# The last feed-forward's down projection as seven half-size products instead of eight, on one Trainium2 core

## What is computed

```python
h = rms_norm(x, norm_ffn[l])
x = x + (jax.nn.silu(h @ w_gate[l]) * (h @ w_up[l])) @ w_down[l]
```

## Time and profile before

| | us |
|---|---|
| median of three runs | 1574.17 |
| the profiled execution, first to last instruction | 1570.6 |
| PE busy in it | 1536.9 (98%) |
| DVE busy | 1007.2 (64%) |
| ACT busy | 832.5 (53%) |
| POOL busy | 210.5 (13%) |

### The profile page before, as it was taken

The page is one execution under the profiler, slowest core; times in us unless marked ns, Lnnn a source line. Parts: engine busy times, 40 slices in busy tenths (PEclk is TensorE's granted clock), DMA queues, the critical chain, the costliest instruction groups (busy, mean ns, idle before and its releaser), DMA issues.

```text
span 1570.6 us, 20022 instructions
## 1 busy us (share of the span) xinstructions
PE 1536.9 (98%) x7872; PEld 1247.3 (79%) x7872; DVE 1007.2 (64%) x1681; ACT 832.5 (53%) x1459; POOL 210.5 (13%) x278
## 2 busy tenths in 40 slices
PE   9999999999999999999989999999999999999999
PEld 8877777788877888888877766888778888888887
DVE  4267977865479998999787786575765333434231
ACT  5278776554456888888863434435434333333220
POOL 1000014522234000000062101111201000000000
PEclk9999999999999999999999999999999999999999
DMA  6122121114547999999943111031212323223232
GB/s 233 65 81 79 56 71 65 54 54 150 214 161 231 375 421 421 421 422 421 326 149 107 54 54 54 28 108 54 81 58 78 108 81 108 92 82 121 67 112 90
DMA packets 78641, 235.89 MB, mean 150 GB/s; under 512 B 6960, under 2 KB 9424, under 8 KB 66256
## 3 DMA queue, kind: packets, MB, share of 16 engines
q1 hardware_dynamic: 68288, 207.62, 36.3%
q10 hardware_dynamic: 6624, 14.88, 2.5%
q0 software_dynamic: 3632, 12.08, 2.0%
HBM read 221.97 MB, written 12.60 MB: 149 GB/s over the span
## 4 chain that ended last, share of the span: by engine, by line
PE 84%; DVE 11%; ACT 2%; issue 1%; DMA 1%; POOL 0%; SPq 0%; DVEq 0%; ACTq 0%; POOLq 0%
PE bank L109 80%; PE bank L112 4%; DVE low L134 2%; DVE REST L124 1%; DVE REST L134 1%; DVE REST L137 1%; ACT REST L115 1%; DVE AL L124 1%; DVE REST L146 1%; DVE REST L143 1%; DVE REST L130 1%; ACT REST L118 1%; ACT CHH L118 0%; DVE R L124 0%; DVE st L140 0%
## 5 line engine op out<-in xcount | busy, mean ns | idle before, releaser
L124 DVE TENSOR_TENSOR low<-slot,CHH 128x1024 fp32r<-128x1024 f32 (+1 forms) x300 | 298.0, 1037 | 117.5 <-ACT CHH L118 116.5
L118 ACT ACTIVATE CHH<-slot 128x1024 fp32r<-128x1024 f32 (+1 forms) x300 | 258.8, 900 | 128.7 <-PE bank L109 56.6
L134 DVE SCALAR_TENSOR_TENSOR low<-slot,smalls,CHH 128x512 fp32r<-128x512 f32 (+1 forms) x232 | 170.3, 766 | 191.2 <-ACT CHH L118 187.3
L109 PE MATMUL bank<-AH,CHH 128*128 128x512 f32 (+1 forms) x640 | 248.5, 388 | 0.2 <-DVE AL L124 0.2
L109 PE MATMUL bank<-AL,CHH 128*128 128x512 f32 (+1 forms) x640 | 242.8, 379 | 0.0
L109 PE MATMUL bank<-AH,low 128*128 128x512 f32 (+1 forms) x640 | 242.6, 379 | 0.0
L118 ACT ACTIVATE CHH<-slot,smalls 128x512 fp32r<-128x512 f32 (+1 forms) x232 | 154.6, 701 | 137.8 <-PE bank L109 68.2
L109 PE MATMUL bank<-CHH,AH 128*128 128x512 f32 x512 | 215.2, 420 | 3.8 <-DVE low L134 2.8
L109 PE MATMUL bank<-low,AH 128*128 128x512 f32 x512 | 200.8, 392 | 0.0
L109 PE MATMUL bank<-CHH,AL 128*128 128x512 f32 x512 | 200.2, 391 | 0.0
L109 PE MATMUL bank<-CHH,XTF 128*128 128x512 f32 x512 | 161.2, 396 | 1.9 <-DVE REST L121 1.1
(11 more groups left out here) (191 smaller groups left out, 2395.4 us busy)
## 6 DMA issues: line engine op xcount, KB each, us to landing
slot<-in_w_in SPq DMA_DIRECT2D x35, 1024.0 KB, 5.1
slot<-in_w_exp_gate SPq DMA_DIRECT2D x32, 1024.0 KB, 13.0
slot<-in_w_exp_up SPq DMA_DIRECT2D x32, 1024.0 KB, 13.2
slot<-in_w_exp_down SPq DMA_DIRECT2D x32, 1024.0 KB, 13.2
slot<-in_w_gate SPq DMA_DIRECT2D x10, 1024.0 KB, 4.9
slot<-in_w_up SPq DMA_DIRECT2D x10, 1024.0 KB, 5.0
slot<-in_w_down SPq DMA_DIRECT2D x10, 1024.0 KB, 5.1
slot<-in_w_out SPq DMA_DIRECT2D x8, 1024.0 KB, 5.1
```

The source lines that it names most:

```text
L109: return self.e.matmul(out, l, r, start=start, stop=stop) if self.e else Issued()
L118: return self.e.activation(out, in_, ACT.Copy, scale=scale) if self.e else Issued()
L124: return self.e.tensor_tensor(out, a, b, op) if self.e else Issued()
L134: return self.e.scalar_tensor_tensor(out=out, in0=a, scalar=s, in1=b, op0=op0, op1=op1) if self.e else Issued()
```

## The change

The operands of the down projection are cut in halves: a into A11, A12, A21, A22 (256 tokens by 1408 features each), w_down into B11, B12, B21, B22 (1408x512 each). Winograd's form of Strassen's scheme needs seven products of halves where eight stood. Each has 11 chunks, 2 token tiles and 3 matmuls: 66 matmuls, six on each chunk.

- **Sums of a.** GpSimd forms S3 = A11-A21, S1 = A21+A22, S2 = S1-A11 and S4 = A12-S2, feature tile by feature tile (128x256), while gate and up run. The high parts of A12, S3, S2, A22, S1 and S4 are then single ScalarE copies of 128x2816 each; the low parts are single subtractions of the same size, S3's and S2's on GpSimd, the other four on VectorE. A11 goes tile by tile.
- **Sums of w_down.** For each of 11 row tiles, one load of 1 MB brings all four quarters (256 rows of 1024 columns). VectorE forms T3 = B22-B12 (`third`), GpSimd then T2 = T3+B11 and T4 = B21-T2. For 11 more tiles B11 and B12 are loaded again, and GpSimd forms T1 = B12-B11.
- **Order on TensorE.** P1 = A11 B11 (chunks 0 to 10), P2 = A12 B21 (11 to 21), then 11 rounds of S2 T2 onto P1's banks (P6), S3 T3 (P7) and A22 T4 (P4) (22 to 54), then S1 T1 onto the same banks (P5, 55 to 65), and S4 B22 (P3, 66 to 76). VectorE adds banks to the residual rows in between. P6 waits for P1's adds, and P5 waits for P6's.
- **Slots.** From chunk 22 five slots take turns (9, 10 and the three of before); slot 9 is first loaded when the gates are done, slot 10 when P1 is done.

```diff
+    plan_block(0, 0)
+    plan_block(1, 0)
+    down_turns = itertools.cycle((9, 10, next(in_turn), next(in_turn), next(in_turn)))
...
+    for j in range(FK):
+        s = plan_slot(next(down_turns), down_rows[:, :, j, :], 2, 1024, 3)
...
+        for name, q, raw_at, low_at in (("T2", 0, b11, b12), ("T3", 0, b22, b22), ("T4", 1, b21, b21)):
...
+    for k in range(0, FK, 2):
...
+        s = plan_slot(next(down_turns), down_rows[:, 0, k:k + m, :], m, 1024, 3)
...
+            formed[c] = ("T1", k + q)
...
+    plan_block(1, 512)
```

On TensorE:

```diff
-        for n in range(2):
-            drain(seg(f"wd{n}", aT, lambda k, j: ("aT", k)))
+        def product(name, c, part, k, two, first, last):
+            hi, lo = high(c), low(c)
+            pe.wait_ge(*at(("part", part, k) if part == A11 else ("part", part)))
+            pe.wait_ge(*at(("", "lo", c)))
+            for i in range(2):
+                l = [x[:, k, i * P:(i + 1) * P] for x in (part_high[part], parts_low[:, part])]
+                pe.matmul_on(two[i], l[0], hi, first, False)
+                pe.matmul_on(two[i], l[1], hi, False, False)
+                m = pe.matmul_on(two[i], l[0], lo, False, last)
...
+        for i in range(2):
+            pe.wait_ge(*at(("on x", "P1", i, 0)))
+        for k in range(FK):
+            c = D0 + 2 * FK + 3 * k
+            product("P6", c, S2, k, sums, False, k == FK - 1)
+            product("P7", c + 1, S3, k, own7, k == 0, k == FK - 1)
+            product("P4", c + 2, A22, k, own4, k == 0, k == FK - 1)
+        for i in range(2):
+            pe.wait_ge(*at(("on x", "P6", 2 + i, 0)))
+        for k in range(FK):
+            product("P5", D0 + 5 * FK + k, S1, k, sums, False, k == FK - 1)
```

On ScalarE and VectorE (`beside[n]` runs after the split of chunk n+5):

```diff
+        beside = {0: lambda: high_of(A12, gates_done, ("a", FT - 1)), 2: lambda: high_of(S3, gates_done, ("S3", FK - 1)),
+                  5: lambda: high_of(S2, ("a", FT - 1), ("S2", FK - 1)), FK + 1: lambda: high_of(A22, ("", "done", D0 + FK - 1)),
+                  2 * FK + 2: lambda: high_of(S1, ("", "done", D0 + 2 * FK - 1)), 2 * FK + 6: lambda: high_of(S4, ("S4", FK - 1))}
...
+        beside = {0: lambda: first_low(FK - 1), 1: lambda: low_of(A12), FK + 1: lambda: add_on("P1", 0, 0),
+                  FK + 3: lambda: low_of(A22), 2 * FK + 1: lambda: add_on("P2", 0, 0, left=True, done=True), 2 * FK + 5: lambda: low_of(S1)}
+        for k in range(FK):
+            beside[2 * FK + 3 * k - 8] = lambda k=k, other=beside.get(2 * FK + 3 * k - 8): (other and other(), third(k))
+        end = 5 * FK
+        for n in range(7 * FK):
+            split_chunks(ahead(D0 + n, 5))
+            if n in beside:
+                beside[n]()
+            if n == end - 1:
+                add_on("P6", 1, 0, bank="P1")
...
+            if n == end + 3:
+                low_of(S4)
```

On GpSimd:

```diff
+        for part in (S3, S2):
+            pool.wait_ge(*at(("part high", part)))
+            pool.wait_ge(*at(("S4", FK - 1)))
+            pool.tt(parts_low[:, part], parts[:, part], part_high[part].bitcast(F32), ALU.subtract).then_inc(*mark("pool_down", ("part", part)))
...
+        for k in range(FK):
...
+            pool.wait_ge(*at(("T3", k)))
+            pool.tt(b11, t3, b11, ALU.add).then_inc(*mark("pool_down", ("T2", k)))
+            pool.wait_ge(*at(("T2", k)))
+            pool.tt(b21, b21, b11, ALU.subtract).then_inc(*mark("pool_down", ("T4", k)))
+        for k in range(FK):
...
+            pool.wait_ge(sem(f"w_land{s.i}"), s.landed)
+            pool.tt(b12, b12, b11, ALU.subtract).then_inc(*mark("pool_down", ("T1", k)))
```

More of the change, by code:

```diff
@@ L25 @@
 FT = 22
+FK = 11
+FH = 256
 EPS = 1e-6
@@ L1395, in tensor, with pair @@
             drain(seg(f"fu{f}", h2, all_of("n4")))
-        for n in range(2):
-            drain(seg(f"wd{n}", aT, lambda k, j: ("aT", k)))
+        def product(name, c, part, k, two, first, last):
[7 more added lines that the diff above has]
+                m = pe.matmul_on(two[i], l[0], lo, False, last)
+                ev = [("full", name, i)] if last else []
+                if i == 1:
+                    ev.append(("", "done", c))
+                if ev:
+                    m.then_inc(*mark("slot_free" if i == 1 and ends_slot(c) else "pe_dense", *ev))
+        def pair(name):
+            two = [banks.use("main", (name, i)) for i in range(2)]
+            for _, old in two:
+                pe.wait_ge(*at(old))
+            return [b for b, _ in two]
+        sums = pair("P1")
+        for k in range(FK):
+            product("P1", D0 + k, A11, k, sums, k == 0, k == FK - 1)
+        own2 = pair("P2")
+        for k in range(FK):
+            product("P2", D0 + FK + k, A12, k, own2, k == 0, k == FK - 1)
+        own7, own4 = pair("P7"), pair("P4")
+        for i in range(2):
[9 more added lines that the diff above has]
+            product("P5", D0 + 5 * FK + k, S1, k, sums, False, k == FK - 1)
+        banks.next["main"] += 2
+        own3 = pair("P3")
+        for k in range(FK):
+            product("P3", D0 + 6 * FK + k, S4, k, own3, k == 0, k == FK - 1)
         banks.groups["main"] = (0, 1, 2, 3)
@@ L2973, in up_evac @@
                 f = f0 + j
-                s = sgp.buf(("sg", f))
+                of = A11 if f < FK else A12
                 dve.wait_ge(*at(("full", f"fu{f0}", j)))
                 dve.wait_ge(*at(("fgs", f)))
[L2977 to L2981, removed]
+                dve.tt(parts[:, of:of + 2, f % FK, :], *(x.rearrange("p (t n) -> p t n", t=2) for x in (
+                    sgp.buf(("sg", f)), banks.ap((f"fu{f0}", j)))), ALU.mult).then_inc(
+                    *mark("dve_evac", ("a", f), ("free", (f"fu{f0}", j)), ("free", ("sg", f))))
+                if f > FK:
+                    first_low(f - FK - 1)
             if f0:
@@ L2985, in vector, with low_of @@
             drain(seg(f"fu{f0}", up_evac))
[L2986 to L2993, removed]
+        def low_of(part):
+            dve.wait_ge(*at(("part high", part)))
+            dve.wait_ge(*at(("S4", FK - 1)))
+            dve.tt(parts_low[:, part], parts[:, part], part_high[part].bitcast(F32), ALU.subtract).then_inc(
+                *mark("dve_evac", ("part", part)))
@@ new lines, in third, with add_on @@
+        def third(k):
+            s, _ = quarters[k]
+            dve.wait_ge(sem(f"w_land{s.i}"), s.landed)
+            dve.tt(s.ap[:, 1, 512:1024], s.ap[:, 1, 512:1024], s.ap[:, 0, 512:1024], ALU.subtract).then_inc(
+                *mark("dve_down", ("T3", k)))
+        last_on = {(i, n): ("x4", i, n) for i in range(NT) for n in range(2)}
+        def add_on(name, half, n, bank=None, left=False, done=False):
+            for i in range(2):
+                to = 2 * half + i, n
+                xs = xr[:, to[0], n * 512:(n + 1) * 512]
+                dve.wait_ge(*at(("full", name, i)))
+                dve.wait_ge(*at(last_on[to]))
+                last_on[to] = ("on x", name, *to)
+                events = [last_on[to]]
+                if left:
+                    events.append(("free", (name, i)))
+                if done:
+                    events.append(("out", *to))
+                dve.tt(xs, banks.ap((bank or name, i)), xs, ALU.add).then_inc(*mark("dve_evac", *events))
```

103 lines of the change are left out of this document (88 added, 15 removed).

## The result

The change makes the kernel slower: 1594.26 us, median of four runs (1592.27 to 1596.69), against 1574.97 us for the kernel before beside it. The ratio is 1.0129, with a 95% interval of 1.0113 to 1.0145. The prediction was 1592 us. The profiled execution spans 1590.4 us, 19.8 more than that of before.

A forecast was written before the change was run, and what follows sets the result against it. TensorE bounds the kernel before; after the change VectorE and GpSimd take turns at SBUF. -15.0 matmuls, +12.2 stage 1, +17.4 stage 3 and border, -0.2 rounding, +3.6 clock: +18, median 1592 us; range 1583 to 1601.

The forecast's parts named there:

- Matmuls: Down projection on TensorE: 66 fewer matmuls at 0.227 us each, saving 15.0 us.
- Stage 1: Chunks 0 to 10: GpSimd's two long low parts hold up VectorE's, making chunk 8 late by 12.2 us.
- Stage 2: Chunks 8 to 24: 17.1 us of shared VectorE and GpSimd work fits in 21.8, so no further loss.
- Stage 3 and the border: Chunk 24 to P5's start: rounds need 4.6 us against 4.08; chunk 55 29.6 us late, 17.4 beyond stage 1.
- Stage 4: P5 and P3, 22 chunks: VectorE's and GpSimd's remaining work fits by little, so no added loss.
- The clock: After stalls in stage 1 and at the P6-P5 border, TensorE runs slow: 3.6 us, bounds 0 to 5.0.
- The sum: Whole kernel: -15.0, +12.2, +17.4, -0.2 rounding and +3.6 clock make +18 us, a median of 1592.
- The floor of +8.8: Down projection if shared access never idles: chunk 55 at 98.8, end at 128.7, the smallest loss, +8.8 us.
- the door: SBUF access shared by VectorE's two-SBUF-input instructions and all GpSimd work; each waits for the other's whole instruction; chance 0.75.
- Rival A: Down projection: VectorE and GpSimd hardly share access, so each engine's work fits; faster, 1561 us; chance 0.09.
- rival B: Down projection: only the long low parts cost, T2, T4 and T1 find gaps; no change, 1574 us; chance 0.09.
- rival C: Rounds: queued loads make T3 wait and block low parts; +10 on the forecast, 1602 us; chance 0.05.

The follow-up runs named there:

- run 10: Changed kernel with all low parts and w_down sums on VectorE, long low parts whole, sums one per chunk, bank adds moved: 1566.59 us, 0.9942 of before.
- Run 2: Changed kernel without the two long low parts of S3 and S2 (high parts read in their place): 1585.25 us, 1.0062 of before.
- run 1: Changed kernel with GpSimd's two long low parts (S3, S2) split into eleven 128x256 subtractions each: 1591.91 us, 1.0109 of before.
- run 4: Changed kernel with GpSimd's 33 sums T2, T4, T1 replaced by subtractions on three different tiles, results unused: 1595.16 us, 1.0128 of before.
- run 6: Changed kernel with T3 formed on GpSimd instead of VectorE: 1601.27 us, 1.0157 of before.
- run 5: Changed kernel with GpSimd's sums T2, T4 and T1 left out, chunks taking the loaded quarters: 1576.20 us, 1.0007 of before.
- run 3: Changed kernel with GpSimd's 33 sums replaced by subtractions on one scratch tile, results unused: 1585.09 us, 1.0066 of before.

## Why the prediction was right

The forecast's mechanism and its sum both held. What it had wrong is where TensorE would stand still, and its smaller terms. The measured lateness of 34.3 us is 13.6 (c8) + 2.05 (clock, c8 to c10) + 17.1 (c24 to c55) + 1.55 (clock, from c55); the forecast had 12.2 + 17.4 + 3.6 of clock = 33.2.

- **Matmuls, -15.0.** 66 fewer, at 0.23 us each where nothing stalls. Right; run 10 shows the gain when it isn't eaten.
- **Stage 1, +12.2.** Measured 13.6 for c8. The order was as written: A12's low part, S3's on GpSimd, c7's, S2's, c8's. GpSimd's hold was 6.0, not 6.2. The rest was a late start: the six small sums took 5.8 us, not the 3.7 that I had from a row with one tile as input and output, and ended at t = 7.7 instead of 6.3, so that A12's low part ended at 11.2 where I had 9.5. TensorE was idle for 7.9 and 3.7 us where I had 6.8 and 5.4: c7's six matmuls, at half the clock, filled more of the second wait. The Trainium skill (SBUF — State Buffer, section "SBUF: two separate sides", which says it for two SBUF inputs in so many words) has the shared pair held for the whole instruction. The trace agrees beyond the 3.88 us that rows of before showed: the low part behind a hold of 6.0 took 6.62, and none got in sooner.
- **Stage 2, no further loss.** Right: 15.6 late from c10 to c28.
- **Stage 3 and the border, +17.4.** c24 to c55 was to take 59.5 us of passages; it took 59.2, with rounds of 4.60 and 26 passages of GpSimd (I had 24 to 27). Adding up the passages was the right model, though it hid where TensorE would stand still: I named one stall of some 5 us at c55. In truth 7.5 of the 17.1 us come at c29 to c35, 4.1 of them at c33, where S1's long low part takes what was left of the lead of five chunks at one stroke, and the stall at c55 was 8 us.
- **Stage 4, no loss.** Right, but for the clock.
- **The clock, +3.6.** The two falls that I had foreseen cost 2.05 and 1.55, together 3.6. I had taken 3.6 between bounds of 0 and 5.0 with no reason for that figure, so the hit is luck. I had missed a third fall, 1.7 us behind S1's stall; it is inside the 17.1 and adds nothing to it. In the first stretch of rows 10 the granted clock stands at 1.00, so the half clock that I read there rested on the spacing of the matmuls alone.
- **The sum.** Down projection 139.2 where I had 134.3 + 3.6 = 137.9; the span +19.8 where I had +18.
- **The floor of +8.8** was called the least that the door allows. Run 2 and run 1 show what it left out: c24 to c55 takes 58.7 and 59.4 us wherever c24 starts. With the lead of at most five chunks, time won early is not saved up, and each stretch pays its own.
- **Rival A** is refuted by the low parts of 6.62 and 1.40 us and by runs 4 and 6, **rival B** by the rounds of 4.60 us, **rival C** by run 5.

## What to carry to other kernels

Before work is moved to an idle engine, ask what both engines read through: additions and subtractions of SBUF tiles on GpSimd and VectorE are one resource here, so the second engine took 1.10 us of it for each sum that the first would have done in 0.60. Add up passages over a stretch to get its length, but look along the queue for the instruction that is longer than the lead that is left. When a chain of waits and a sum of passages give the same number, only a run with the work kept and the data taken out of it tells them apart, and the stand-in must have the same operands, not only the same size.

## What the runs showed of the hardware beyond the forecast

- GpSimd's subtraction of 128x512 with one tile as both inputs and as output is quicker than with three different places: 1.46 against 1.70 us on average in the turns (runs 3 and 4), and VectorE's low parts beside it take 1.26 instead of 1.44. The real sums, with two different inputs and the output on one of them, take 1.76, so it is not the separate output that costs.
- A stall need not be long for a slow stretch to follow. In run 10 TensorE stood still for 2.0 us; the granted clock in two stretches behind it:

```profile
1485.50:1488.50 3.00, 1.02 (x5) 0.87 (x6) 3.00 (x6) 1.69 (x3) 0.00 (x0) 1.00 0.55 225
1488.70:1491.00 2.30, 2.30 (x7) 1.72 (x6) 2.30 (x5) 0.63 (x2) 0.00 (x0) 0.50 0.35 36
```

  The clock was still at 2.4 GHz while TensorE started again, and at 1.2 GHz 1.2 us later, with TensorE busy all the time: 1.7 us of lateness from c24 to c27. Run 2's stall of 2.0 us was followed by such a stretch too.
